# A two-layer block on one core: tokens on partitions for the output projections, the second FFN product and the residual, and three of eight low parts of each norm on GpSimd

## The reference

```
for layer in range(2):
    sh_m, sc_m, g_m, sh_f, sc_f, g_f = split(silu(c) @ ada_w[layer] + ada_b[layer], 6)
    h = rms_norm(x, norm_w[layer, 0]) * (1 + sc_m) + sh_m
    y = even_mixer(h) if layer == 0 else odd_mixer(h)      # both end in y @ w_out
    x = x + g_m * rms_norm(y, norm_w[layer, 1])
    h = rms_norm(x, norm_w[layer, 2]) * (1 + sc_f) + sh_f
    a, g = split(causal_conv3(h @ ffn_in_w[layer]) + conv_b, 2)
    x = x + g_f * rms_norm((a * gelu(g)) @ ffn_out_w[layer], norm_w[layer, 3])
```

## Time and profile before

| | |
|---|---|
| median of 3 runs | 2669.17 us (2665.86 to 2672.18) |
| the profiled execution, its own time | 2670.19 us |
| its span in the profile | 2668.3 us |
| mean granted clock of TensorE | 0.963 |
| busy: PE, DVE, ACT, POOL | 2466.6, 2020.0, 1078.5, 462.8 us |
| moved by DMA | 631.37 MB |

### The profile page before, as it was taken

One profiled execution on the slowest core, in us unless ns is written; L12 is line 12 of the kernel. 1 busy time (PEld: TensorE's weight loads), 2 busy tenths in 40 slices (PEclk: granted clock), 3 DMA queues, 4 the chain that ended last, 5 costly groups with the idle time before them and its releaser, 6 DMA issues.

```text
span 2668.3 us, 47925 instructions
## 1 busy us (share of the span) xinstructions
PE 2466.6 (92%) x18998; PEld 2389.3 (90%) x18998; DVE 2020.0 (76%) x2394; ACT 1078.5 (40%) x1111; POOL 462.8 (17%) x230
## 2 busy tenths in 40 slices
PE   1399998979999999999979999988999999999997
PEld 1398877969999999999979989987999999999997
DVE  7877887779987999789777766677998456645655
ACT  1334334454333333333464544544434333433344
POOL 0100000013430344024210000000444024401420
PEclk7699998989999999999989999989999999999998
DMA  9887774857778777887757644366577455555453
GB/s 397 327 318 288 280 248 148 278 180 262 270 280 317 288 268 278 309 297 270 251 190 263 227 154 147 142 233 237 209 274 260 174 188 175 187 175 186 178 182 132
DMA packets 114781, 631.37 MB, mean 237 GB/s; under 512 B 12752, under 2 KB 12880, under 8 KB 62944
## 3 DMA queue, kind: packets, MB, share of 16 engines
q1 hardware_dynamic: 114656, 629.61, 64.8%
HBM read 627.46 MB, written 2.10 MB: 236 GB/s over the span
## 4 chain that ended last, share of the span: by engine, by line
PE 81%; DVE 9%; DMA 5%; ACT 2%; issue 2%; POOL 1%; DVEq 0%; SPq 0%; ACTq 0%; POOLq 0%
PE bank L1422 24%; PE bank L1423 23%; PE bank L1424 23%; DMA piece<-ada_pieces 3%; PE bank L1441 2%; PE bank L1443 2%; PE bank L1442 2%; DVE lo L805 1%; DVE region L816 1%; DMA region<-ada_pieces 1%; PE bank L1329 1%; DVE piece L816 1%; ACT hi L439 1%; DVE act L866 1%; DVE region L836 1%
## 5 line engine op out<-in xcount | busy, mean ns | idle before, releaser
L1422 PE MATMUL bank<-act,hi 128*128 128x256 f32 x4384 | 1261.3, 288 | 112.3 <-DVE act L866 96.8
L439 ACT ACTIVATE hi<-raw 128x2048 fp32r<-128x2048 f32 x402 | 769.6, 1915 | 1301.9 <-PE bank L1424 1174.6
L1423 PE MATMUL bank<-act,hi 128*128 128x256 f32 x4384 | 1247.9, 285 | 0.0
L1424 PE MATMUL bank<-act,lo 128*128 128x256 f32 x4384 | 1247.6, 285 | 0.0
L805 DVE TENSOR_TENSOR lo<-raw,hi 128x2048 fp32r<-128x2048 f32 x402 | 920.8, 2290 | 193.6 <-ACT hi L439 192.7
L1422 PEld LDWEIGHTS bank<-act,hi 128*128 128x128 f32 x4384 | 849.1, 194 | 122.3 <-issue 108.0
L1423 PEld LDWEIGHTS bank<-act,hi 128*128 128x128 f32 x4384 | 849.7, 194 | 1.0
L1424 PEld LDWEIGHTS bank<-act,lo 128*128 128x128 f32 x4384 | 849.0, 194 | 0.0
L816 DVE SCALAR_TENSOR_TENSOR piece<-piece,cond 128x1024 f32<-128x1024 f32 x320 | 451.4, 1411 | 78.2 <-DMA piece<-ada_pieces 77.9
L1422 PE MATMUL bank<-mid,hi 128*128 128x256 f32 x1408 | 406.6, 289 | 13.3 <-POOL mid L789 13.3
L1423 PE MATMUL bank<-mid,hi 128*128 128x256 f32 x1408 | 400.5, 284 | 0.0
(11 more groups left out here) (150 smaller groups left out, 1516.6 us busy)
## 6 DMA issues: line engine op xcount, KB each, us to landing
raw<-w_units SPq DMA_DIRECT2D x402, 1024.0 KB, 4.8
piece<-ada_pieces SPq DMA_DIRECT2D x320, 512.0 KB, 4.8
region<-ada_pieces SPq DMA_DIRECT2D x64, 512.0 KB, 8.7
x<-x_in SPq DMA_DIRECT2D x1, 2048.0 KB, 16.3
x_out<-x SPq DMA_DIRECT2D x4, 512.0 KB, 2.6
cond<-c_row SPq DMA_DIRECT2D x1, 1024.0 KB, 4.9
vec<-vectors SPq DMA_DIRECT2D x1, 534.5 KB, 11.8
extra<-blocks_in SPq DMA_DIRECT2D x1, 512.0 KB, 18.4
```

The source lines that it names most:

```text
L439: sc.activation(hi[:, slot, :], raw[:, raw_slot, :], ACT.Copy).then_inc(s_hi, 1)
L1422: pe.matmul(dst, w_hi, src[:, kt, 0:T], start=at == 0, stop=False)
L1423: pe.matmul(dst, w_hi, src[:, kt, T:2 * T], start=False, stop=False)
L1424: i_ = pe.matmul(dst, w_lo, src[:, kt, 0:T], start=False, stop=at == len(order) - 1)
```

## The change

Output projections (`mixed`) and `ff_down` use the token form; `ff_down`'s third group is 12 full units in place of 16, so there are 394 units. x and y lie with tokens on partitions, in memory too. A mean over channels is then ACT's `accum_out` of a square, and the factor of a token is one value for each partition. Gamma, however, must lie along the row: ACT stores its 2048 values to a scratch row and loads that broadcast, in units 5 and 6 of the phase. For the projections x is turned by PE: 32 fp32 matmuls of 128 x 128 against a diagonal that holds the tokens' factors; ACT and DVE scale and shift out of PSUM, ACT makes high parts, and of the eight low parts (two tiles each) DVE makes five and POOL three. The gates move into the first five units of the output projection. Some modulation pieces move to other units.

```
+        self.k_units = len(range(0, FF_GROUPS[group], 4)) if kind == "ff_down" else 4
+        self.tokens = kind in ("values", "mixed", "ff_down")
+    def token_unit(self, j):
+        if self.kind == "mixed":
+            return j % 2, tail(self)[0][j // 2], j < 2, j >= 6
+        tile, g = divmod(j, self.k_units)
+        return tile, g, g == 0, g == self.k_units - 1
...
-              Phase("columns", 0, 4, 4, (2, 1, 2, 1), dest=FQ),
+              Phase("columns", 0, 4, 4, (2,) * 4, dest=FQ),
-              Phase("mixed", 0, 4, 4, (2, 1, 2, 1)),
-              Phase("ff_up", 0, 8, 4, (1,) * 4, 0), Phase("ff_down", 0, 4, 4, (2, 1, 2, 1), 0),
+              Phase("mixed", 0, 2, 8, (0, 1, 0, 0, 1, 2, 2, 2)),
+              Phase("ff_up", 0, 8, 4, (1,) * 4, 0), Phase("ff_down", 0, 2, 8, half, 0),
-              Phase("ff_up", 0, 6, 4, (1,) * 4, 2), Phase("ff_down", 0, 4, 4, (1, 0, 1, 0), 2),
+              Phase("ff_up", 0, 6, 4, (1,) * 4, 2), Phase("ff_down", 0, 1, 12, (1, 2, 1) * 4, 2),
-              Phase("mixed", 1, 4, 4, (2, 1, 2, 1)),
+              Phase("mixed", 1, 2, 8, (0, 0, 0, 0, 1, 2, 2, 3)),
...
+X_PIECES = ((0, 0, 1024), (0, 1024, 1024), (1, 0, 1024), (1, 1024, 512), (1, 1536, 512))
+LOW_VECTOR, LOW_POOL = (0, 1, 2, 4, 6), (3, 5, 7)
...
         # ScalarE
+            def square_x(q):
+                for k, (tb, at, size) in enumerate(X_PIECES):
...
+                    sc.activation(yt[:, tb, at:at + size], x[:, tb, at:at + size], ACT.Square,
+                                  accum_out=stat[:, col:col + 1]).then_inc(s_xsq, 1)
+            def gamma_row_dmas(ph, j):
+                if j == 5:
+                    sc.wait_ge(s_gamma, m + 1)
+                        sc.dma_start(row_dram.rearrange("a (k p) -> p (a k)", p=P), gamma[:, :]).then_inc(s_row_out, 16)
+                if j == 6:
+                    sc.wait_ge(s_row_out, 16 * (m + 1))
+                    sc.dma_start(gamma_row, row_dram.broadcast_to([P, D])).then_inc(s_row, 16)
+            def gate_work(ph, j):
+                if ph.layer == 0 and j == 3:
+                    gated_to_act(ph, 0)
+                    gated_to_act(ph, 1)
...
         # GpSimd
+                    for p in LOW_POOL:
+                        gp.wait_ge(s_hh, 8 * q + p + 1)
+                        gp.tensor_tensor(act[:, 2 * p:2 * p + 2, T:2 * T], y[:, 2 * p:2 * p + 2, :],
+                                         act[:, 2 * p:2 * p + 2, 0:T].bitcast(F32), ALU.subtract).then_inc(s_actp, 1)
...
         # VectorE
+            def by_gamma(ph, chunk, first=0, last=TB):
+                if chunk == 0:
+                    ve.wait_ge(s_row, 16 * (m + 1))
+                ve.wait_ge(s_ysq, TB * CHUNKS * m + TB * chunk + last)
+                ve.tensor_tensor(yt[:, first:last, at], yt[:, first:last, at],
+                                 gamma_row[:, at].unsqueeze(1).broadcast_to([P, last - first, 512]),
+                                 ALU.mult).then_inc(s_yg, 1)
+            def post_norm(ph, between):
+                by_gamma(ph, CHUNKS - 1, 0, 1)
+                ve.wait_ge(s_ysq, TB * CHUNKS * (m + 1))
+                ve.tensor_reduce(r, split2(stat[:, S_Y:S_Y + TB * CHUNKS]), AX_X, ALU.add).then_inc(s_mean, 1)
+                by_gamma(ph, CHUNKS - 1, 1, 2)
+                between()
+                rooted(r)
+                for tb, at, size in X_PIECES:
+                    ve.scalar_tensor_tensor(out=x_at, in0=yt[:, tb, at:at + size], scalar=r[:, tb:tb + 1], in1=x_at,
+                                            op0=ALU.mult, op1=ALU.add).then_inc(s_x, 1)
+            def pre_norm(ph):
+                for p in (1, 3):
+                    scaled(p)
+                for p in (0, 1):
+                    low(p)
+                scaled(5)
+                low(2)
+                scaled(7)
+                for p in (4, 6):
+                    low(p)
+            def gate_work(ph, j):
+                if ph.layer == 0:
+                    if j == 0:
+                        low_part(ph, 3)
+                    if j == 1:
+                        mlstm_normed(1, 0)
+                    if j == 2:
+                        mlstm_normed(1, 1)
+                        gate(ph, 0)
+                    if j == 3:
+                        low_part(ph, 0)
+                        gate(ph, 1)
+                    if j == 4:
+                        low_part(ph, 1)
...
+                        if ph.tokens and complete:
+                            for tb in range(TB):
+                                tok_ps = bank[2 * (tile_no % 2) + tb][:, :]
+                                elif ph.kind == "ff_down" and ph.group > 0:
+                                    i_ = ve.tensor_tensor(yt[:, tb, at_], yt[:, tb, at_], tok_ps, ALU.add)
+                                else:
+                                    i_ = ve.tensor_copy(yt[:, tb, at_], tok_ps)
+                            i_.then_inc(s_evac, 1)
+                            if ph.sums and ph.tiles * i + tile > 0:
+                                by_gamma(ph, ph.tiles * i + tile - 1)
...
         # TensorE
+            def x_transposes(q, p):
+                if p >= 4 and p % 2 == 0:
+                    pe.wait_ge(s_na, 4 * q + (p - 4) // 2 + 1)
+                if p >= 4 and p % 2 == 1:
+                    pe.wait_ge(s_nv, 4 * q + (p - 4) // 2 + 1)
+                for kt in (2 * p, 2 * p + 1):
+                    for tb in range(TB):
+                        i_ = pe.matmul(bank[4 + p % 4][:, at:at + P], x[:, tb, kt * P:(kt + 1) * P], diag[:, tb, :],
+                                       start=True, stop=True)
...
+                    pe.wait_ge(s_diag, q + 1)
+                    for p in range(6):
+                        x_transposes(q, p)
+                            if kt in (2, 4):
+                                x_transposes(q, 5 + kt // 2)
```

More of the change, by code:

```diff
@@ L446, in split_next, with root @@
                       m // RAW_SLOTS + i * (ph.units // RAW_SLOTS) + 1)
-            sqp = Tally(s_sqp)
-            ysq = Tally(s_ysq)
-            xup = Tally(s_x)
             means = Tally(s_mean)
-            def root(at_, scale=1.0):
+            def root(at_, scale=1.0, bias=0.0):
                 sc.wait_ge(s_mean, means.step())
[L455 to L461, removed]
@@ L463, in pre_norm, with token_root @@
-            def pre_norm(layer, part, first):
-                for b in range(4):
-                    if xup.at == 0:
+                sc.activation(at_, at_, ACT.Sqrt, bias=bias, scale=scale).then_inc(s_root, 1)
+            def token_root(at):
+                root(stat[:, at:at + TB], 1.0 / D, stat[:, S_EPS:S_EPS + 1])
+            def square_x(q):
+                for k, (tb, at, size) in enumerate(X_PIECES):
+                    if q == 0:
                         sc.wait_ge(s_in["x"], 16)
@@ new lines, in gamma_row_dmas @@
+            def gamma_row_dmas(ph, j):
+                m = 2 * ph.layer + int(ph.kind == "ff_down")
+                if j == 5:
+                    sc.wait_ge(s_gamma, m + 1)
+                    with nc.allow_non_contiguous_dma("2048 values, once for each norm"):
+                        sc.dma_start(row_dram.rearrange("a (k p) -> p (a k)", p=P), gamma[:, :]).then_inc(s_row_out, 16)
+                if j == 6:
+                    sc.wait_ge(s_row_out, 16 * (m + 1))
+                    sc.dma_start(gamma_row, row_dram.broadcast_to([P, D])).then_inc(s_row, 16)
@@ L1166, in body @@
                         after_split(ph, i, j)
+                        if ph.kind == "mixed" and first_body(i):
+                            gate_work(ph, j)
+                            if j == 4:
+                                gate_weight(ph.layer, 0)
+                        if ph.kind == "columns" and ph.side == "gla" and i == ph.bodies - 1 and j == ph.units - 1:
+                            mixer = PHASES[PHASES.index(ph) + 1]
+                            gate(mixer, 0)
+                            gate(mixer, 1)
                         if ph.ada[j] > 0:
@@ L1515 @@
         w = (even_out_w, odd_out_w)[layer][0]
-        for m in range(DK):
-            units[n] = columns_unit(w, slice(m * P, (m + 1) * P))
-            n += 1
+        rows = row_units(w)
+        mixer = next(ph for ph in PHASES if ph.kind == "mixed" and ph.layer == layer)
+        for i in range(mixer.bodies):
+            for j in range(mixer.units):
+                chunk, group = mixer.token_unit(j)[0:2]
+                units[n] = rows[mixer.tiles * i + chunk, group]
+                n += 1
         first = 0
@@ L1525 @@
                     n += 1
-            rows = ffn_out_w[layer][first * P:(first + tiles) * P]
-            for m in range(DK):
-                units[n][:, 0:tiles * P] = columns_unit(rows, slice(m * P, (m + 1) * P))
-                n += 1
+            got = row_units(ffn_out_w[layer][first * P:(first + tiles) * P]).reshape(-1, P, UNIT)
+            units[n:n + len(got)] = got
+            n += len(got)
```

548 lines of the change are left out of this document (281 added, 267 removed).

## The result

The changed kernel takes 2651.23 us, the median of 5 runs (2648.88 to 2657.25), beside 2667.0 for the kernel before in the same session: ratio 0.9939, 95% interval 0.992 to 0.9958. It is faster, by 16 us and not by 90. The profiled execution took 2648.88 us, its span is 2647.1.

A forecast was written before the change was run, and what follows sets the result against it. TensorE, busy 92% of the span, bounds the kernel, so time comes from fewer or cheaper matmuls and its gaps. 24.8 + 16.8 + 16.8 + 19.1 + 14.2 - 1 = 90.7 saved from 2670.2 gives 2579.5, forecast 2579 us; range 2554 to 2612.

The forecast's parts named there:

- 5.44 a unit in token form: Output projections and FFN second products: 24 matmuls of 512 columns, 5.46 us a unit, 87.4 for 16 units.
- a first seam of 2.7: Ahead of the first output projection: unit 0 needs only chunk 2, so the seam of 11.8 becomes 2.5 us.
- 16.0 us from the diagonal: Inner norms: 17 us from the diagonal to the end of the next phase's first unit.
- a tail of 12.6 against 12.2: Kernel's end: the tail loses the first passes, 17.9 becomes 12.2 us, 5.7 saved.
- From the end of unit 5: high split 1.9 before the load is issued, load 4.9 ...: Last FFN groups: with product 1.2 and low split 2.3, 10.3 us where TensorE wants unit 7 at 5.5.
- A stall of 8: Each last FFN group: 4.9 us of stall, 1 for a busy DMA, 2 for the clock.
- The rival that named this store: Last FFN groups and output projections: gamma's 2048-value store lands slowly, 98 us and 14 for the clock, 2675 us; chance 0.04.
- SyncE's weight and piece loads keep their order and lose eight.: Last FFN groups: ScalarE's queue carries gamma's two transfers, SyncE's queue only loses eight loads.
- ... so between 0 and 16 x 0.45 = 7 lost; I take 2.: First projection: two pieces a unit make each buffer's cycle 6.2 against 5.76 us; 2 us lost.
- 94.9 and 96.9: First and second output projections: 2.5 + 87.4 plus waits of 5 and 7 us; 16.8 and 19.1 saved.
- the norms' 14.2 us: Norm seams, start and tail together: 14.2 us saved.
- the low parts: Norms: GpSimd's low parts taken at 1.5 us; rival has them wait on VectorE, 4.7 each, 2616 us, chance 0.12.

The follow-up runs named there:

- e10_64bytes: The changed kernel with gamma stored as it lies, 128 runs of 64 bytes, right order left out; load unchanged; 2621.34 us, one execution.
- e1_rows: The changed kernel with gamma turned by TensorE and stored as 16 rows of 512 bytes, and made in unit 0 of the output projections; 2618.51 us, ratio 0.9818.
- e3_sp: The changed kernel with SyncE waiting, ahead of the second output projection, for the last GLA product instead of the last head's stored result; 2646.2 us, ratio 0.9911.
- e6_mlstm: The changed kernel with eight pieces moved from the first projection to the mLSTM's phase; 2639.21 us, ratio 0.9907.
- all mended: The changed kernel with gamma in 16 rows, made, stored and loaded earlier, SyncE's shorter wait, pieces moved to the mLSTM and within the second output projection; 2572.78 us.

## Why the prediction was wrong

The direction and the mechanism of the gain were right: 5.44 a unit in token form, 86.8 for 16 units against 87.4 forecast, a first seam of 2.7, 16.0 us from the diagonal (made by 1378.9) to the end of the norm's unit (1394.9) against 17, a tail of 12.6 against 12.2. Of the 69 us that are missing, 48 to 56 belong to three steps.

*"From the end of unit 5: high split 1.9 before the load is issued, load 4.9 ..."* This step of the last FFN group left the store's own time out: the load waits for the store to land, and goes out 15.2 us after it in layer 0, and itself lands in 8.3 (median). A stall of 8 became 18.4 and 16.1 (the two units behind it, 29.3 and 27.0, less twice 5.44). With 64-byte runs both groups are 73.6, against 73.5 forecast, but that agreement is in part luck. In layer 1 of that run TensorE waits 5.7 (forecast 4.9 and 1), and the unit behind the wait takes 2.7 more than 5.44 (forecast 2 for the clock, whose grant is 0.60 from 2575 to 2580); but the load goes out with the high split (2566.35 beside 2566.33), not 1.9 behind it, and takes 7.5, not 4.9. In the output projections, where I had put nothing for the store, its form alone took 5.6 and 3.1 (`e10_64bytes`); with gamma made earlier as well it was 8.5 and 8.9 (`e1_rows`). There ScalarE's queue, with the load waiting in it, stood 7.8 and 6.0. Together 27 to 35 us.

The rival that named this store priced it by the value (0.24 us, from the mean packet of 4 to 8 KB) and made it 31 us, deciding from 0.23. The runs show no such price, and the slowdown that it forecast did not come either; 0.04 was too little for a cost that no row before bounded more closely than 0 and 31. I chose the end near 0 and gave the range no part of the middle. The Trainium skill, DMA: Bandwidth & Descriptors, Rules for kernel authors, says that a non-contiguous last dimension becomes one descriptor per element and is better rearranged. The trace agrees: the queue of gamma's transfers moved 8832 packets, and 1152 with the 64-byte runs, 4 x (2048 - 128) fewer. The Trainium skill, on the same page, Specifications, says that under 512 bytes a transfer is a read, a change and a write; by that rule the 64-byte runs should stand with the single values, and the runs put them with the rows (4.5 against 4.4 us), so the size alone does not carry the difference.

*"SyncE's weight and piece loads keep their order and lose eight."* This was written for the FFN, and not checked for the second output projection. The order is kept, but a wait in it now waits for unit 3: 8.9 us (`e3_sp`). The change moved GLA's last norm, and the queue that waits for it was not followed.

*"... so between 0 and 16 x 0.45 = 7 lost; I take 2."* The mechanism was right, only the size off: a buffer's cycle is 1.2 for the sum and 5.2 for the load in that stretch, not 4.8, together 6.4, near the 6.47 that a unit took. That lost 10.8 in all, and 3.3 in the phase behind (`e6_mlstm` gives nearly all of it back).

Of the other 13 to 21 us, 8 to 16 are in the output projections, in the waits for pieces and gates and for gamma's making, which no run parts: with all mended, the projections stand at 99.2 and 100.2 against 94.9 and 96.9, so those waits were put 3 to 4 us too low each. Of the norms' 14.2 us 11.6 came; the low parts were on neither side of it. GpSimd's take 1.54 us, as taken. The Trainium skill, SBUF — State Buffer, Who interferes with whom, has a VectorE instruction with two SBUF inputs contend with a GpSimd instruction that reads SBUF; VectorE's 0.685, which becomes 1.096 in the mean beside GpSimd, agrees. What the share given to GpSimd gains is too little to be measured. That 2572.78 lies near the 2579 forecast is no credit to the forecast: it is another kernel, with the row fetched in time.

## What to carry to other kernels

A store whose reader waits is priced from issue to landing and from landing to the next landing, and one of single values is avoided (turn the tile first, or store it in runs) or issued long before anyone waits: its cost falls on every transfer in flight, and on the engine in whose queue the load waits. When a step is moved, look for every queue that waits for its semaphore, those of loads above all. Work that fills a buffer is best put beside units that are long for another reason, and its cycle is buffer sum plus landing in that very stretch.

## What the runs showed of the hardware

A store of 256 to 2048 single values took 9.9 to 13.6 us to land (medians), against 4.5 for 128 runs of 64 bytes; only some 4 us of that go with the number. With 2048 the other transfers were held at 19 to 57 GB/s for 12 us. A broadcast load in runs of 1 KB took 19.7 us (one execution) where one in runs of 8 KB took 8.3. And a VectorE subtraction of 128 x 512 took 1.57 us beside a GpSimd one, 0.64 alone.
